# Seven products for the third block's tile pairs as well, all weight sums in the second block, and the next x loaded after the last gates

## The reference

```python
h = rmsnorm(x, g_pre[l])
proj = h @ w_in[l]                       # 1024 x 10240
# twelve parts of 512 columns, for four branches, and 4 x 1024 gate logits
out_a = gmlp_spatial(a_u, v_n, w_s[l], b_s[l]) * silu(a_z)      # chunks of 128 frames
out_b = silu(layernorm(causal_depthwise(ext_b, conv_b_w[l]) + ...)) * silu(b_z)   # 31 taps
out_c = multiscale_pool(ext_c, ...) * silu(c_z)                 # windows 2, 4, 8, 16
out_d = d_b * causal_depthwise(ext_d, conv_d_w[l]) * silu(d_z)  # 3 taps
gates = sigmoid(gate_logits + b_gate[l])
merged = sum over the branches of gates[k] * (out_k @ w_branch[l, k])   # 512 x 1024 each
y = merged @ w_out[l]
x = x + rmsnorm(y, g_post[l])
```

## Time and profile before

| | |
|---|---|
| median of three runs | 2390.71 us |
| the profiled execution: span from first to last instruction | 2389.8 us |
| TensorE matmul busy | 2376.6 us, 12340 matmuls |
| VectorE, ScalarE, GpSimd busy | 1478.7, 431.1, 598.4 us |
| moved by DMA | 647.03 MB, mean 271 GB/s |
| blocks, from the first unit of each | 0 to 583, 583 to 1160, 1160 to 1737, 1737 to 2390 us |

### The profile page before, as it was taken

The page is one execution under the profiler, slowest core; times in us unless marked ns, Lnnn a source line. Parts: engine busy times, 40 slices in busy tenths (PEclk is TensorE's granted clock), DMA queues, the critical chain, the costliest instruction groups (busy, mean ns, idle before and its releaser), DMA issues.

```text
span 2389.8 us, 32530 instructions
## 1 busy us (share of the span) xinstructions
PE 2376.6 (99%) x12340; PEld 2063.3 (86%) x12340; DVE 1478.7 (62%) x2155; ACT 431.1 (18%) x629; POOL 598.4 (25%) x323
## 2 busy tenths in 40 slices
PE   9999999999999999999999999999999999999998
PEld 7888888888888888888888888888898999999998
DVE  7886877853666556654275655674237776677643
ACT  5223222323011111121212111111010110011111
POOL 4435545455222222212332222322100000000000
PEclk9999999999999999999999999999999999999999
DMA  8977888797975878777786777767564458988884
GB/s 327 317 253 279 309 295 287 270 336 284 359 263 220 307 255 307 281 253 270 294 303 230 281 288 290 299 229 271 211 243 180 145 190 280 332 283 269 281 275 180
DMA packets 168895, 647.03 MB, mean 271 GB/s; under 512 B 15360, under 2 KB 16768, under 8 KB 123712
## 3 DMA queue, kind: packets, MB, share of 16 engines
q1 hardware_dynamic: 156416, 612.85, 71.4%
q10 hardware_dynamic: 12352, 32.49, 3.7%
HBM read 474.82 MB, written 170.46 MB: 270 GB/s over the span
## 4 chain that ended last, share of the span: by engine, by line
PE 94%; DVE 3%; issue 1%; DMA 1%; DVEq 1%; POOL 0%; ACT 0%; ACTq 0%; SPq 0%; POOLq 0%
PE acc L1802 65%; PE acc L2016 10%; PE side L2027 4%; PE side L1940 4%; PE acc L2166 3%; PE side L2166 3%; PE side L2016 2%; PE acc L1907 1%; PE side L1968 1%; PE acc L2163 1%; PE side L2163 1%; PE side L1958 1%; DMA w_pair<-split_main 0%; DVE cb L1094 0%; PE acc L2202 0%
## 5 line engine op out<-in xcount | busy, mean ns | idle before, releaser
L1802 PE MATMUL acc<-h_hi,w_pair 128*128 128x512 f32 (+1 forms) x4384 | 1262.7, 372 | 0.6 <-DMA w_pair<-split_main 0.5
L1802 PEld LDWEIGHTS acc<-h_hi,w_pair 128*128 128x128 f32 x4384 | 789.9, 188 | 140.8 <-issue 1.2
L1802 PE MATMUL acc<-h_lo,w_pair 128*128 128x512 f32 (+1 forms) x2192 | 780.0, 371 | 0.0
L1802 PEld LDWEIGHTS acc<-h_lo,w_pair 128*128 128x128 f32 x2192 | 400.4, 188 | 68.6
L1094 DVE SCALAR_TENSOR_TENSOR cb<-glu,col,cb 128x512 f32<-128x512 f32 x600 | 443.2, 803 | 21.8 <-issue 15.2
L566 POOL TENSOR_TENSOR w_pair<-w_raw,w_pair 128x1024 fp32r<-128x1024 f32 x118 | 268.0, 2284 | 272.5 <-ACT w_pair L696 257.4
L1802 PE MATMUL acc<-out_hi,w_pair 128*128 128x512 f32 (+1 forms) x800 | 258.5, 386 | 1.5 <-DVE tmp L1399 1.5
L599 POOL TENSOR_TENSOR rstd<-msq,nhalf 128x5 f32<-128x5 f32 (+4 forms) x19 | 20.3, 1069 | 694.4 <-DVE msq L1020 531.9
L590 POOL TENSOR_TENSOR s_lo<-w_raw,s_hi 128x1024 fp32r<-128x1024 f32 x50 | 127.2, 2567 | 238.9 <-ACT s_hi L707 238.9
L1802 PEld LDWEIGHTS acc<-out_hi,w_pair 128*128 128x128 f32 x800 | 149.0, 188 | 32.3 <-DVE tmp L1399 2.3
L757 ACT ACTIVATE sig<-acc,col 128x512 f32<-128x512 f32 (+1 forms) x98 | 67.6, 690 | 590.5 <-PE acc L1802 588.4
(11 more groups left out here) (296 smaller groups left out, 2779.4 us busy)
## 6 DMA issues: line engine op xcount, KB each, us to landing
w_pair<-split_main SPq DMA_DIRECT2D x206, 1024.0 KB, 5.1
split_main<-w_pair SPq DMA_DIRECT2D x88, 1024.0 KB, 6.7
w_raw<-in_w_main SPq DMA_DIRECT2D x138, 512.0 KB, 5.5
chunk<-s_parts SPq DMA_DIRECT2D x100, 512.0 KB, 6.1
chunk<-split_main SPq DMA_DIRECT2D x75, 512.0 KB, 6.0
w_pair<-split_branch SPq DMA_DIRECT2D x66, 512.0 KB, 4.2
s_parts<-s_hi SPq DMA_DIRECT2D x25, 1024.0 KB, 6.0
s_parts<-s_lo SPq DMA_DIRECT2D x25, 1024.0 KB, 8.3
```

Of the source, the lines that this page charges most:

```text
L1802: ins = pe.matmul(acc[:, s, b, 0:m], wt[slot][:, wk], mv_[:, k, t0:t0 + m], start=(k == 0 and n == 0), stop=(k == nk - 1 and n == 2))
```

## The change

`SEVEN0 = 2`: the third and the fourth block (`is_seven`) take the seven products. Their weights come in one stream of chunks (`chunk_stream`): the third block's pairs and its O units, then the fourth block's units up to G0's first four, and its pairs. `t_hi`, `t_lo`, `t_sum`, `half`, `quarters` and `banks` exist for each of the two widths; a product has 256 columns in the third block.

All weight sums are made in the second block, by halves: half `h` is every other run of 256 columns of a pair (`src[:, hx::2, :]`), in one of three buffers, `s_raw` and `s_sum`, whose space the high and low parts reuse. SP issues loads and stores at the two-unit slots `HALF_LOAD` and `HALF_STORE`, ScalarE casts behind the units `HALF_CAST`, GpSimd works in the order of `HALF_POOL`.

x rows of the next block go to `x_half`, in the space of `out_hi[1]` and `out_lo[1]`, loaded once G1 is done. x itself goes to the space of `h_lo` (`h_x`), loaded after the last gate's sigmoid; the row of scales is copied out of PSUM (`h_row_copy`), and all eight tiles are scaled after the last merge (`x_scale_all`). The casts of h follow two a unit in O. The first step of O takes all eight banks.

The core of the diff:

```diff
-TURN = (NCHUNK - 1) % CHUNKS // 2 + 1
-SUM_AT = [0, 2, 4, 6, 8, 10, 12, 14, 16, 18, 20, 24, 26]
+SEVEN0 = 2
+NH = 2 * NPAIR
+HW = WB // 2
+HALF_LOAD = [h * 29 // 25 for h in range(NH)]
+HALF_CAST = [max(0, 2 * s - 1) for s in HALF_LOAD]
+HALF_STORE = [s + 2 for s in HALF_LOAD]
+HALF_POOL = [2 * s for s in HALF_LOAD]
...
+def chunk_stream():
+
+    stream, pair_at, unit_at, counted, last_of = [], {}, {}, 0, []
+
+    def put(src, done):
+        stream.append(src)
+        last_of.append(done)
+
+    for j in range(SEVEN0, NBLK):
+        if j > SEVEN0:
+            for name, count in SECTIONS:
+                for r in range(4 if name == "G0" else count):
+                    u = j * UPB + UNIT0[name] + r
+                    unit_at[u] = len(stream)
+                    for piece in unit_pieces(name, r):
+                        put(piece, ("unit", u + 1))
+                if name == "G0":
+                    break
+        for p, (name, q) in enumerate(PAIRS):
+            pair_at[j, p] = len(stream), counted
+            g = PAIR_TILE[p]
+            srcs = [("main", g, 0), ("sum", p, 1), ("sum", p, 2), ("sum", p, 0), ("main", g, 1), ("sum", p, 3),
+                    ("main", g + 1, 1)]
+            if name[0] == "G":
+                srcs += [("branch", GATED[name][0] * KT + 2 * (q + (name == "G0")) + t, 0) for t in range(2)]
+            for src in srcs:
+                counted += 1
+                put(src, ("chunk", counted))
+        if j < NBLK - 1:
+            for k in range(KT):
...
+                u = j * UPB + UNIT0["O"] + k
+                unit_at[u] = len(stream)
+                for piece in unit_pieces("O", k):
+                    put(piece, ("unit", u + 1))
+    return stream, last_of, pair_at, unit_at
...
+    h_x = sb("h_x", [P, KT, WMAX], addr=at[0])
...
+    x_half = [sb(f"x_half{h}", [P, TPB // 2, DM], addr=o) for h, o in enumerate(out1_at)]
...
+    half_at = [raw_at, raw_at + 8 * HW * 4, a + 2 * WMAX * 4 + EL * 4]
+    s_raw = [sb(f"s_raw{b}", [P, 4, HW], addr=o) for b, o in enumerate(half_at)]
+    s_hi = [sb(f"s_hi{b}", [P, 4, HW], F32R, addr=o) for b, o in enumerate(half_at)]
+    s_sum = [sb(f"s_sum{b}", [P, 4, HW], addr=o + 4 * HW * 4) for b, o in enumerate(half_at)]
+    s_lo = [sb(f"s_lo{b}", [P, 4, HW], F32R, addr=o + 4 * HW * 4) for b, o in enumerate(half_at)]
...
-        t_sum[t] = sb(f"t_sum{t}", [P, CT, WMAX // 2], addr=t_at[2 * n + 1])
...
+            t_at = [raw_at, raw_at + part, xr_at, raw_at + 2 * part] + [xr_at + n * part for n in (1, 2, 3)] + [bs_at]
...
+        def s_load(h):
+
+            q, hx, b = h // 2, h % 2, h % 3
+            if h >= 3:
+                sp.wait_ge(s_stored[b], 32 * (h // 3))
+            for t in range(2):
+                src = raw_rows(PAIR_TILE[q] + t).rearrange("p (c n) -> p c n", c=4)
+                sp.dma_start(s_raw[b][:, 2 * t:2 * t + 2, :], src[:, hx::2, :]).then_inc(s_loaded[b], 16)
...
+        def s_store(h):
+
+            q, hx, b = h // 2, h % 2, h % 3
+            sp.wait_ge(s_lo_done, h + 1)
+            for n, part in enumerate((s_hi[b], s_lo[b])):
+                dst = s_parts[q, :, n, :].rearrange("p (c n) -> p c n", c=8)
+                sp.dma_start(dst[:, hx::2, :], f(part)).then_inc(s_stored[b], 16)
...
+        def load_chunk(n):
+
+            if n < CHUNKS:
+                sp.wait_ge(acc_done, SEVEN0 * UPB + SEVEN_AT - RING + n // 2 + 1)
             else:
-                sp.wait_ge(s_stored, 32 * q)
-            for t in range(2):
-                sp.dma_start(w_raw[t][:, :], raw_rows(PAIR_TILE[q] + t)).then_inc(s_loaded, 16)
...
+        for j in range(1, SEVEN0 + 1):
+            for name, count in SECTIONS:
+                if is_seven(j) and name == "D":
+                    break
+                for r in range(4 if is_seven(j) and name == "G0" else count):
+                    u = UNIT0[name] + r
+                    if j == 1 and u % 2 == 0:
+                        for h in range(NH):
+                            if HALF_STORE[h] == u // 2:
+                                s_store(h)
+                            if HALF_LOAD[h] == u // 2:
+                                if h == 0:
+                                    sp.wait_ge(w_lo_done, UPB)
+                                s_load(h)
+                    (kind, m, _), *more = unit_pieces(name, r)
+                    if more:
...
+                for b in range(3):
+                    sp.wait_ge(s_stored[b], 32 * ((NH + 2 - b) // 3))
+            load_chunk(n)
...
+        def s_half(h):
+
+            b = h % 3
+            a11, a12, a21, a22 = (s_raw[b][:, c, :] for c in range(4))
+            pool.wait_ge(s_loaded[b], 32 * (h // 3 + 1))
+            pool.tensor_tensor(s_sum[b][:, 2, :], a21, a11, ALU.subtract)
             pool.drain()
-            pool.tensor_tensor(s2, s1, a11, ALU.subtract)
...
+            pool.tensor_tensor(s_sum[b][:, 1, :], a22, s_sum[b][:, 2, :], ALU.add)
...
-            pool.tensor_tensor(s4, a12, s2, ALU.subtract)
...
             pool.drain().then_inc(s_summed, 1)
...
+            pool.tensor_tensor(s_lo[b][:, :, :], s_sum[b][:, :, :], f(s_hi[b])[:, :, :],
+                               ALU.subtract).then_inc(s_lo_done, 1)
 
...
+
+            if j == 1:
+                for h in range(NH):
+                    if HALF_CAST[h] == u - j * UPB:
+                        act.wait_ge(s_summed, h + 1)
+                        act.activation(s_hi[h % 3][:, :, :], s_sum[h % 3][:, :, :], ACT.Copy).then_inc(s_hi_done, 1)
...
+                copy_p1(j, p)
+                if (name, q) == ("G2", 0) and j < NBLK - 1:
+                    load_x_rows(j + 1)
...
+            if j < NBLK - 1:
+                act.drain().then_inc(z_sig_ready, 2 * CT)
+                load_x(act, j + 1)
...
                 act.wait_ge(cpy_used, j * 8 + 8)
+                gates("G1", 24)
+                act.wait_ge(acc_done, ub + UNIT0["G2"])
                 load_x_rows(j + 1)
-                gates("G1", 24)
                 gates("G2", 32)
...
-            if not last:
+            if not is_seven(j):
                 gates("G2b", 46)
-                act.wait_ge(x_summed, j + 1)
+                gates("G3", 48)
                 load_x(act, j + 1)
...
+        def h_row_copy(j):
+
+            k = SIDE["H", j]
+            dve.wait_ge(side_done, k + 1)
+            dve.tensor_copy(h_row[:, 0:width(j)], side[:, k % 2, 0:width(j)])
+            dve.drain().then_inc(side_free, 1)
+
+        def x_scale_all(j):
+
+            dve.drain()
+            for k in range(KT):
+                if k % 2 == 0:
+                    dve.wait_ge(x_loaded[k // 2], 16 * (j + 1))
+                x_scaled(j, k, 0)
...
                     split_merged(m)
+                if name == "G2" and not last:
+                    x_stats(m)
...
+                if not last:
+                    x_mean_squares()
                 for q in range(4):
-                    pair_sums(p + q)
+                    pair_sums(p + q, (lambda: h_row_copy(j + 1)) if q == 2 and not last else None)
                     for t in range(2):
                         seven_merge(p + q, t)
+                    if q == 0 and not last:
+                        rstd_diag(j + 1)
                 dve.drain().then_inc(sig_used, SEVEN_SIGS)
+                if not last:
+                    dve.drain().then_inc(cpy_used, CT)
+                    x_scale_all(j + 1)
...
+                wk = slice(k % CT * P, (k % CT + 1) * P)
+                if j > SEVEN0:
+                    if k % CT == 0:
+                        landed(UNIT_AT[u] + k // CT)
+                    w_k = chunk[(UNIT_AT[u] + k // CT) % CHUNKS]
+                else:
...
+                    if name == "G3" and q == 2 and not last:
+                        pe.wait_ge(pair_used, 2 * g)
+                        row_job(j + 1, kh)
```

More of the change, by code:

```diff
@@ new lines, in _, with body @@
+        for name, count in SECTIONS:
+            u0 = UNIT0[name]
+            def body(i, like=0):
+                for r in range(4):
+                    tick(u0 + i * 4 + r, r, u0 + like * 4 + r)
+            n = count // 4
+            if name in ("B", "C", "O"):
+                for r in range(count):
+                    tick(u0 + r, r, u0 + r)
+                    if name == "B" and 2 <= r < 6:
+                        h_part(0, 2 * (r - 2))
+                    if name == "C" and r == 1:
+                        power(n=TPB)
+                    if name == "O":
+                        h_part(1, r)
+            elif n == 1:
+                body(0)
+            elif name == "G2":
+                each(pool, 0, n - 1, body)
+                for r in range(4):
+                    tick(u0 + 4 * n - 4 + r, r, u0 + 4 * n - 4 + r)
+                    if r == 1:
+                        power(TPB + 1)
+            else:
+                first = int(name == "G3")
+                if first:
+                    body(0)
+                    power(TPB + 1)
```

(25 more changed lines are left out.)

575 lines of the change are left out of this document (263 added, 312 removed).

## The result

The changed kernel takes 2377.06 us (median of 4 runs, 2375.72 to 2379.08) against 2390.78 us for the kernel before (2390.61 to 2391.86): ratio 0.9942, 95% interval 0.9928 to 0.9956. The profiled execution has a span of 2377.0 us.

What follows compares the result with a forecast made beforehand. Taken as bound by PE's own issue rate. Against the 2389.8 us span, -22.1 - 0.6 + 6 + 2 + 2 + 1 = -11.7 gives 2378.1, or 2379 as timed median; range 2366 to 2398.

Steps and rivals of the forecast that it cites:

- Seven products: Third block: 84 matmuls of 256 columns replace 48 of 512 per pair, 10.88 to 10.00 us, x 25 = -22.1 us.
- Rival 3: Third block: 256-column matmuls cost what 288 do, paced by weight loads; +6.2 in place of -22.1, 2405 us; chance 0.05.
- Sums leaving the third block: Third block: its 12 pairs' weight sums go, and with them PE's idle behind a late weight load; -0.6 us (0 to -1.3).
- Sums in the second block: Second block: all 50 halves share the weight-load queue and overfill the 32 gate slots; +6 us, ends 0 and +122.
- 8.36 us a slot, 0.20 too long, x 32: Second block's gate slots: transfers at 52 ns per 1 KB packet take 8.36 us against PE's 8.16; +6 us.
- Rival 1: Second block becomes bound by its transfers, deciding from 56.3 ns a packet; at 60 ns, 2401 us; chance 0.17.
- Entry: Third block's first pairs: VectorE's chain, 27.7 us, outlasts PE's 26.0 us of work, so PE waits; +2 us (0 to 4).
- Chunks of the D pairs: Third block: chunk loads take 10.73 us a pair, 0.73 late; over 8 pairs, less 3.8 slack, +2 us (0 to 5.8).
- 342 when full: Third block's D pairs: full DMA rate of 342 GB/s, from the fourth block's 332 at share 0.97; 10.73 us a pair.
- x rows in the third block: Third block: next x rows (2 MB), moved to the first G2 pair, cost 6.1 us less slack and catching up; +1 us.
- x behind the last gates: Loads of x behind G3's sigmoids, then scalings during the output projection, hidden by 12 us; cost 0.
- Rival 2: All is hidden: packets at 48 to 50 ns, chunks keep up by slack, VectorE's lag vanishes; 2368 us; chance 0.24.

Runs made afterwards that it cites:

- the kernel with the old third block: The changed kernel with the seven products in the fourth block alone, weight sums still wholly in the second block: 2397.31 us, ratio to before 1.0025.
- Holes there: The changed kernel with no weight-sum halves loaded in slots 2, 3, 34, 39, 40, 41 and 51, where SP issues beside row loads: 2372.67 us, ratio 0.9922.
- the kernel with holes and entry: The changed kernel with weight sums kept out of slots where row loads are issued, and sigmoid and merge moved earlier at the pairs' entry: 2368.95 us, ratio 0.9907.
- the kernel with one hole: The changed kernel with only the two halves of slots 38 and 39 moved to free slots 28 and 36: 2374.47 us, ratio 0.9930.

## Why the prediction was right, and where it was not

The sum was -11.7 us of span, and it came to -12.8; median 2377.1 against 2379. That the two lie so close is in part luck: gains and losses that the sum missed, of up to 2.8 us each, cancel. By its steps:

- **Seven products, -22.1.** 25 x (10.88 - 9.92) = -24.0; the line through 288 and 512 columns was 0.9 ns a matmul too dear. Rival 3 (256 columns cost what 288 do) falls. Against the kernel with the old third block the net is -19.3: the entry takes 2.1 us, three further waits (0.4 us at 1484, 0.8 at 1559, 0.5 at 1631) 1.7, and 0.9 us lie in pieces too small to place.
- **Sums leaving the third block, -0.6.** -1.9 us with the other moves, more than the bound of 1.3. I can't part them.
- **Sums in the second block, +6.** +8.8, or +6.6 by the shortest of the five profiles. The size was near by luck; the step "8.36 us a slot, 0.20 too long, x 32" failed. The 1 KB packet that it took at 52 ns lasted 48.7 on average in this block, under the 49.6 up to which a slot fits, so by its own sum the term was 0, and G0 and D show no wait of 0.3 us. What it missed is that a transfer on another queue in the same microseconds, which the prediction let fall "into full slots", is nearly the whole cost: 5.9 us in one place, 2.1 in another. Holes there took off 7.4 of the 8.8 us. Rival 1, which begins at 56.3 ns, falls with it: the share was 0.93 over the block, and a stretch moved 414 GB/s. (The Trainium skill, DMA: Bandwidth & Descriptors, "Where 436 GB/s comes from", has HBM bind a core at some 358 GB/s; that stretch does not agree.)
- **Entry, +2.** 2.1 us, but not since VectorE's work is longer than PE's: the same work in another order leaves no wait. The size was right and its reason wrong.
- **Chunks of the D pairs, +2.** 0. The step "342 when full" failed: 361 GB/s came. Then a pair's 3.67 MB take 10.17 us against 9.92, 2 us over eight pairs, inside the slack of 3.8.
- **x rows in the third block, +1.** 0 by the same slack; with 2.8 us less of it, 4.0 us of waits came up there, and slow matmuls behind them.
- **x behind the last gates, 0.** Right, by the margin given (12 us): GpSimd's last low parts below end at 1717.45, PE takes the first at 1730.14.

```profile
1714.62 2.83 POOL L691 TENSOR_TENSOR h_lo<-h_x,h_hi 128x576 fp32r<-128x576 f32 x2 [2.72 <-ACT h_hi L877]
```

Rival 2 (2368) was not what happened, since the waits did not vanish by themselves. That the kernel with holes and entry comes to 2369 is because they were taken away.

## What to carry to other kernels

An average load under the engines' limit says little where a queue carries bulk traffic ahead of tiles that are due: look for the moments at which another queue adds its own burst, and keep the bulk out of the slots that are *issued* then. They run ahead of the compute by the ring's depth, here four units. Where PE waits at the entry to a stage, read the order on the two engines that feed it before counting their work.

## What was not expected of the hardware

Behind a wait of PE the granted clock fell to the 1.2 GHz level for some microseconds, which adds nearly half to the price of the wait: 4.0 us cost 5.9. Behind waits of 1.2 and 2.1 us it stayed at 1.00, behind those of 2.9 us and more in these runs it fell each time. One of 2.0 us, in the kernel with one hole, was followed by a fall too, so the length of the wait alone does not decide it:

```profile
987.00:991.00 4.00, 4.00 (x14) 3.15 (x13) 0.08 (x1) 0.34 (x1) 3.44 (x3) 0.68 0.73 283
```
